# The small expert's up sums: four plain transposes and one VectorE addition in place of products with a constant tile

## The reference

```python
def swiglu(h, w_gate, w_up, w_down):
    a = jnp.einsum('bsd,df->bsf', h, w_gate)
    b = jnp.einsum('bsd,df->bsf', h, w_up)
    return jnp.einsum('bsf,fd->bsd', jax.nn.silu(a) * b, w_down)

def moe_swiglu(h, router, w_gate, w_up, w_down):
    ...
    for e in range(N_EXPERTS):
        y = y + combine[..., e:e + 1].astype(h.dtype) * swiglu(h, w_gate[e], w_up[e], w_down[e])
    return y
```

## Time and profile before

| | |
|---|---|
| median of 3 runs | 1382.0 us (1379.66, 1382.15, 1382.0) |
| the profiled execution | 1379.63 us |
| its span, first to last instruction | 1377.5 us |
| mean granted TensorE clock | 0.998 of full speed |
| moved by DMA | 433.21 MB, 314 GB/s over the span |

### The profile page before, as it was taken

The page is one execution under the profiler, slowest core; times in us unless marked ns, Lnnn a source line. Parts: engine busy times, 40 slices in busy tenths (PEclk is TensorE's granted clock), DMA queues, the critical chain, the costliest instruction groups (busy, mean ns, idle before and its releaser), DMA issues.

```text
span 1377.5 us, 19168 instructions
## 1 busy us (share of the span) xinstructions
PE 1357.2 (99%) x6673; PEld 1095.3 (80%) x6673; DVE 1115.4 (81%) x970; ACT 959.1 (70%) x904; POOL 13.7 (1%) x26
## 2 busy tenths in 40 slices
PE   9999999999999999999999999999999999999997
PEld 7888888888788787877787777787777778787775
DVE  6566544455555789999999999999999999999997
ACT  6554533333454478888887888877888887888886
POOL 1100000000000000000000000000000000000000
PEclk9999999999999999999999999999999999999999
DMA  9813555555351059999999999998999998999993
GB/s 375 319 58 110 212 185 186 194 193 187 131 228 39 17 205 420 422 422 421 422 382 352 421 422 422 422 421 335 399 421 422 422 422 352 379 422 422 422 422 151
DMA packets 61398, 433.21 MB, mean 314 GB/s; under 512 B 7066, under 2 KB 7241, under 8 KB 10032
## 3 DMA queue, kind: packets, MB, share of 16 engines
q1 hardware_dynamic: 59312, 426.80, 76.7%
q0 software_dynamic: 1888, 5.78, 1.2%
q10 hardware_dynamic: 160, 0.14, 0.0%
HBM read 431.60 MB, written 1.09 MB: 314 GB/s over the span
## 4 chain that ended last, share of the span: by engine, by line
PE 95%; DVE 2%; ACT 2%; issue 1%; ACTq 0%; DVEq 0%
PE ps L1453 20%; PE ps L1454 19%; PE ps L1455 19%; PE ps L1851 7%; PE ps L1850 7%; PE ps L1861 4%; PE ps L1862 4%; PE ps L1889 4%; PE ps L1582 1%; PE ps L1786 1%; PE ps L1555 1%; PE ps L1460 1%; PE ps L1853 1%; PE ps L1854 1%; PE ps L1897 1%; PE ps L1823 1%
## 5 line engine op out<-in xcount | busy, mean ns | idle before, releaser
L909 DVE TENSOR_TENSOR wlo<-raw,whi 128x2048 fp32r<-128x2048 f32 (+1 forms) x403 | 905.1, 2283 | 126.1 <-PE ps L1455 90.7
L539 ACT ACTIVATE whi<-raw 128x2048 fp32r<-128x2048 f32 (+1 forms) x403 | 759.0, 1912 | 78.4 <-PE ps L1455 66.3
L1453 PE MATMUL ps<-whi,xhi 128*128 128x512 f32 (+1 forms) x880 | 346.2, 393 | 4.9 <-DVE wlo L909 2.3
L1455 PE MATMUL ps<-whi,xlo 128*128 128x512 f32 (+1 forms) x880 | 342.0, 389 | 0.0
L1454 PE MATMUL ps<-wlo,xhi 128*128 128x512 f32 (+1 forms) x880 | 342.0, 389 | 0.0
L1453 PEld LDWEIGHTS ps<-whi,xhi 128*128 128x128 f32 x880 | 165.2, 188 | 42.1 <-DVE wlo L909 5.2
L1455 PEld LDWEIGHTS ps<-whi,xlo 128*128 128x128 f32 x880 | 165.2, 188 | 34.7
L1454 PEld LDWEIGHTS ps<-wlo,xhi 128*128 128x128 f32 x880 | 165.4, 188 | 32.5
L1851 PE MATMUL ps<-wlo,xhi 128*64 128x512 f32 x392 | 155.2, 396 | 0.0
L1850 PE MATMUL ps<-whi,xhi 128*128 128x512 f32 x392 | 153.4, 391 | 0.0
L1453 PE MATMUL ps<-whi,thi 128*128 128x512 f32 x320 | 125.7, 393 | 0.0
(11 more groups left out here) (248 smaller groups left out, 1102.3 us busy)
## 6 DMA issues: line engine op xcount, KB each, us to landing
raw<-in_moe_up SPq DMA_DIRECT2D x112, 1024.0 KB, 7.4
raw<-in_moe_gate SPq DMA_DIRECT2D x112, 1024.0 KB, 8.0
raw<-in_moe_down SPq DMA_DIRECT2D x112, 1024.0 KB, 7.2
raw<-in_ffn_up SPq DMA_DIRECT2D x14, 1024.0 KB, 4.8
raw<-in_ffn_gate SPq DMA_DIRECT2D x14, 1024.0 KB, 4.8
raw<-in_ffn_down SPq DMA_DIRECT2D x14, 1024.0 KB, 4.8
raw<-in_dil_w_in SPq DMA_DIRECT2D x10, 1024.0 KB, 4.7
raw<-in_swa_w_in SPq DMA_DIRECT2D x4, 1024.0 KB, 19.4
```

The lines of the kernel that those rows point to most:

```text
L539: act.activation(whi[:, c % HIS, 0:span(c)], raw[:, c % RAW, 0:span(c)], ACT.Copy).then_inc(hi_ready, 1)
L909: dve.tensor_tensor(wlo[:, c % LOS, 0:n], raw[:, c % RAW, 0:n], whi[:, c % HIS, 0:n].bitcast(F32), ALU.subtract).then_inc(lo_ready, 1)
L1453: pe.matmul(dst, ahi, bhi, start=start, stop=False)
L1455: return pe.matmul(dst, alo, bhi, start=False, stop=stop)
```

## The change

`fold` no longer multiplies the up sums by the constant tile. It turns them with four plain transposes into bank `B_UB`, which the copies have emptied, and signals `up_turned`. On VectorE a new `small_up` adds the two halves of the turned sums with one reduction: it reads all 512 columns of the bank, in pairs that stand 64 apart, and writes 256 numbers to `small_h` in SBUF. `small_mul` reads them there. The gate sums are folded as before. The transposes wait only for the up sums' copy, the gate products for the gate sums'. TensorE gets two more waits for the addition (`up_added`), because bank `B_UB` is in use until then: ahead of the small up products and in `gather`.

```diff
@@ -285,6 +285,7 @@
         halves_set, sums_out, folded = sem("halves_set"), sem("sums_out"), sem("folded")
+        up_turned, up_added = sem("up_turned"), sem("up_added")
@@ -360,6 +361,14 @@
+        def turned_half(bank, half):
+
+            return ps[:, bank, :].rearrange("p (k t) -> p k t", k=FT)[:, :, half * HALF:(half + 1) * HALF]
+
+        def turned_both(bank):
+
+            return ps[:, bank, :].rearrange("p (k two t) -> p k t two", k=FT, two=2)
@@ -1361,10 +1370,16 @@
+            def small_up(pair, s):
+
+                dve.wait_ge(up_turned, STEPS * pair + s + 1)
+                dve.tensor_reduce(small_act(), turned_both(B_UB), mybir.AxisListType.X, ALU.add).then_inc(up_added, 1)
+
             def small_mul(pair, s):
 
                 dve.wait_ge(silu_b, STEPS * pair + s + 1)
-                dve.tensor_tensor(small_h[:, 1, :], small_folded(0), small_h[:, 0, :], ALU.mult)\
+                dve.wait_ge(up_added, STEPS * pair + s + 1)
+                dve.tensor_tensor(small_h[:, 1, :], small_h[:, 1, :], small_h[:, 0, :], ALU.mult)\
                     .then_inc(act_b, 1)
@@ -1394,8 +1409,9 @@
                     large_tlo(pair, s - 1)
-                    for i in range(1, 3):
-                        cut(c + i, rs)
+                    cut(c + 1, rs)
+                    small_up(pair, s - 1)
+                    cut(c + 2, rs)
                     small_mul(pair, s - 1)
@@ -1409,8 +1425,9 @@
                 large_tlo(pair, STEPS - 1)
-                for i in range(1, 3):
-                    cut(MOE0 + PAIR_UNITS - 4 + i, r)
+                cut(MOE0 + PAIR_UNITS - 3, r)
+                small_up(pair, STEPS - 1)
+                cut(MOE0 + PAIR_UNITS - 2, r)
                 small_mul(pair, STEPS - 1)
@@ -1786,6 +1803,8 @@
+                    if kt == 1 and not first:
+                        pe.wait_ge(up_added, STEPS * pair)
                     if kt == KT - 3 and not first:
                         pe.wait_ge(act_b, STEPS * pair)
@@ -1883,11 +1902,14 @@
             def fold(pair, s):
 
+                pe.wait_ge(sums_out, 2 * (STEPS * pair + s) + 1)
+                for j in range(FT):
+                    last = pe.transpose(ps[:, B_UB, j * P:(j + 1) * P], small_sums(0)[:, j, :], ident)
+                last.then_inc(up_turned, 1)
                 pe.wait_ge(sums_out, 2 * (STEPS * pair + s) + 2)
-                for part in range(2):
-                    for j in range(FT):
-                        last = pe.matmul(small_folded(part)[:, j * HALF:(j + 1) * HALF], small_sums(part)[:, j, :],
-                                         both_halves[:, :], start=True, stop=True)
+                for j in range(FT):
+                    last = pe.matmul(small_folded(1)[:, j * HALF:(j + 1) * HALF], small_sums(1)[:, j, :],
+                                     both_halves[:, :], start=True, stop=True)
                 last.then_inc(folded, 1)
@@ -1926,6 +1948,7 @@
+                    pe.wait_ge(up_added, STEPS * pair + s)
                     for i in range(2):
                         small_in(c + 2 + i, rs, B_UB, i)
```

## The result

| | before | after |
|---|---|---|
| median | 1382.08 us | 1369.34 us |
| runs | 1379.66 to 1383.35 (4) | 1368.19 to 1372.31 (4) |
| profiled execution, its span | 1379.63, 1377.5 us | 1369.4, 1367.6 us |

The ratio is 0.9911, with a 95% interval of 0.9899 to 0.9923: 12.3 us less (10.6 to 14.0). 1369 us had been forecast, in a range of 1366 to 1376.

A forecast was written before the change was run, and what follows sets the result against it. TensorE was taken to bound the kernel, VectorE and transfers within 4%. The fold's 11.8 us, minus 0.4 for new waits, plus 0.6 for the gate sums' wait, minus 0.3 at the end, gave 11.7: forecast 1369 us, range 1366 to 1376.

The forecast's parts named there:

- The bound: Expert steps of 29.72 us: TensorE decides, VectorE and the transfers wait for it, all three within 4%.
- The fold: TensorE, each fold: four transposes replace the up half's products, saving 0.42 us (0.38 to 0.44), 11.8 us over 28 folds.
- New waits: TensorE, ahead of the small up products: waiting for the addition costs its issue alone, 0.4 us in all.
- The gate sums' wait: TensorE at four folds: transposes now stand in front of the 0.8 us wait for gate sums, giving 0.6 us back.
- VectorE's reduction: VectorE, each step: adding the halves takes 0.68 us, 0.60 net; work of 29.09 us fits a 29.30 us step.
- Transfers: Weight transfers don't get faster; in the first pair's last step, transfers and cuts are still in time by 0.3 us.
- The later pairs can't have less: Pairs after the first begin after a pause of the transfers, so their reserve is no smaller than 0.3 us.
- Rival A: Expert steps: the transfers bind, so only 5.9 us are gained, 1373.7 us; chance 0.13.
- The end: Last pair: the last transfer's landing and the cuts behind it hold TensorE's last small products, costing 0.3 us once.
- The sum: Whole kernel: all terms together save 11.7 us, 1367.9 us from the profiled execution; forecast 1369 us, chance 0.70.
- B: Loop steps: VectorE binds from a net reduction of 0.81 us on; 2.4 us gained, 1377.2 us; chance 0.10.
- C: Loop steps: a reduction beyond 1.23 us net, from PSUM pairs 64 apart, makes the kernel slower, 1390 us; chance 0.05.

The follow-up runs named there:

- the first run: VectorE's half of the change on the kernel before: old fold on TensorE, plus the reduction, result unused, and TensorE's waits for it; 1382.19 us, ratio 1.0001.
- half transfers on the kernel before: The kernel before with the weight transfers of the experts' steps at half their bytes, every engine operation kept; 1382.21 us, ratio 1.0003.
- second profile: The unmodified changed kernel profiled again beside the last experiment; 854.77 us from the experts' start to TensorE's last expert product, against 853.86 us in its first profile.

## Why the prediction was right, point by point

**The bound.** "TensorE decides, since the other two wait for it" held, before and after. It is shown by the first run (VectorE's half alone changes nothing) and by half transfers on the kernel before.

**The fold, 0.42 us, mis-sized.** The fold itself gave 0.45 us and the whole step 0.465, both above my upper bound of 0.44. The transposes took 0.43 us as predicted (0.44). The error was in the gate half: I let it give back 0.05 us or nothing, and it fell from 0.87 to 0.82 us. At the first fold of all the halves were 0.87 and 0.87 us, and are 0.43 and 0.81. What a group of transposes takes depends on what comes next. It is 0.43 us ahead of narrow instructions (the gate products, or four more transposes), but 0.36 us for the second four in the run with both kinds of sums transposed, and just as short behind wide products, in `large_t`:

```profile
695.24 0.60 PE L1919 MATMUL ps<-mats,act_h 128*128 128x128 f32 x4
695.59 0.48 PE L1880 MATMUL ps<-wlo,thi 128*64 128x512 f32 x1
```

Both of these stand ahead of a product of 512 columns. Why the gate products cost 0.05 us less behind transposes than behind their like stays open; the whole miss of 0.045 us a step is 1.3 us over 28 folds.

**New waits, -0.4 us.** Nothing: TensorE has no idle time in front of the small up products.

**The gate sums' wait, +0.6 us.** Nothing either. The four folds at the pairs' starts, for which the trace gave 0.8 us of waiting in sum, saved 0.43 to 0.52 us each, the same as all others. So the starts show nothing of the wait that the view listed there, beyond 0.04 us a fold (0.87 us for the up half against 0.83). The view of waits has the 0.8 us at the weight loads (`PEld`) and none at the products.

**VectorE's reduction, 0.68 us and 0.60 net.** It lasts 682 ns, as long as the plain operations on 512 elements, and stands 0.60 us from the next start. The sum 28.49 + 0.60 = 29.09 us a step, which leaves 0.16 us of 29.25, was too high all the same: VectorE pauses twice a step in the kernel before, and each pause leaves the end of an instruction (0.08 us) that otherwise overlaps the next one; the busy time 28.49 holds both. By the distance of starts the work with two reductions is 29.48 us (above), so with one it is 28.88 us, and 0.37 us are left. That it was near the edge is shown by the run with two of them.

**Transfers, in time by 0.3 us in the first pair's last step.** This step of the working failed on a small scale: 0.5 us were lost there. Two things had not been put in. The six folds ahead gained 6 x 0.045 = 0.3 us more, which alone used up the margin. And the transfers did not keep their times: the unit that I had followed landed 183.0 us after the experts' first product, where it was 182.4 us, 0.6 us later. The chain behind the landing was as priced: from 685.18 to the end of the second cut at 692.32 pass 7.1 us, against 7.3. It does not contain the addition, and VectorE stood idle for 0.19 us in it. "The later pairs can't have less" held in one profile and not in the other: the time between the end of a cut and its product, at the same unit of the four pairs, was 0.06, 0.34, 0.52 and 0.68 us, and 0.06, 0.05, 1.13 and 0.40 us in the second profile, where the second pair lost 0.56 us as well. Rival A named the right mechanism, but at 5.8 us, where 0.5 to 1.2 us were lost in the loops.

**The end, 0.3 us.** The weakest term: 1.25 us were lost more than before. I had followed the last transfer alone. What decided came earlier: the unit that landed at 1339.12. From 1341.26 on VectorE worked without a gap, through four cuts and four small operations, until the small part was done at 1352.02:

```profile
1341.26 2.29 DVE L918 TENSOR_TENSOR wlo<-raw,whi 128x2048 fp32r<-128x2048 f32 x1 [0.27 <-ACT whi L548]
1343.47 0.68 DVE L1370 TENSOR_TENSOR tlo<-ps,thi 128x512 fp32r<-128x512 f32 x1
1344.07 2.28 DVE L918 TENSOR_TENSOR wlo<-raw,whi 128x2048 fp32r<-128x2048 f32 x1
1346.27 0.68 DVE L1376 TENSOR_REDUCE small_h<-ps 128x256 f32<-128x512 f32 x1
1346.87 2.28 DVE L918 TENSOR_TENSOR wlo<-raw,whi 128x2048 fp32r<-128x2048 f32 x1
1349.07 0.42 DVE L1382 TENSOR_TENSOR small_h<-small_h 128x256 f32<-128x256 f32 x1
1349.41 2.28 DVE L918 TENSOR_TENSOR wlo<-raw,whi 128x2048 fp32r<-128x2048 f32 x1
1351.61 0.41 DVE L1388 TENSOR_TENSOR thi<-small_h,thi 128x256 fp32r<-128x256 f32 x1
```

The chain had to be summed over everything that VectorE does after a landing, not over the last unit.

**The sum.** 11.7 us had been predicted and 11.2 were found in the trace, by terms that missed in both directions: +1.2 for the fold, +0.4 and -0.6 for the waits, -0.5 and -0.95 for the two places. The mechanism was right, and that the sum came out this close is partly luck. The medians moved by 12.7 us, the ratio says 12.3; the rest lies around the span, as said above, and in the spread of its start. The lower edge of the range had a slip: a saving of 0.44 us and no cost of waits give 1366.7 us, and not 1366.5.

**Rivals.** B (VectorE binds) needed a reduction of over 0.81 us net and C (slower) one of over 1.23; at 0.60 both fall. Made true by hand, with the second reduction, B's mechanism appears, but at half its price. Two reductions are 1.20 us net, by my arithmetic a step of 29.69 us in all loops, 24 x 0.44 = 10.6 us above the changed kernel; 4.7 us were measured. The first pair had mostly 29.43 to 29.52 us, the later ones 29.25 us up to their last steps. The lead at a pair's start and the 0.2 us by which 28.49 was too high were not in it.

## What to carry to other kernels

Where three resources stand within about 4% of each other, a saving on the one that decides pays in full only up to the next one's rate. This change kept 11.2 of its 13.0 us in the traces, and the same edit on the gate sums, with the addition that it needs, made the kernel slower. Price an edit by what it adds to the runner-up as well as by what it takes off the leader, and look at the lead in the last step of a loop, where reserves are gone. At the end of a kernel, add up all the work of the engine behind the last few landings; the last transfer alone says too little. And take a second profile of the same kernel before a microsecond is given to a cause.

## What the runs showed of the hardware

- A reduction on VectorE that reads 512 fp32 elements of PSUM as pairs 64 apart and writes 256 took 682 ns, the time of a plain operation on 512 elements (682 and 683 ns). Neither the stride nor the 256 outputs cost anything that can be seen. The Trainium skill (VectorE: DVE Perf Modes, "Rules for kernel authors") calls this operation the slowest of the engine and says to consider restructuring on a hot path; at this shape no run agrees that it is slower than the others.
- A group of four transposes took 0.43 us ahead of narrow products or other transposes, and 0.35 to 0.36 us ahead of a product of 512 columns, to the start of what came next.
- Transfers of 1 MiB landed every 2.487 us (422 GB/s) inside a pair, before and after, but their time from issue to landing grew (median of the down matrix 7.2 us before, 9.2 after) without one more byte: a transfer issued sooner waited longer behind the others. So a longer time to landing was here no sign of slower transfers.
- The start of the experts' stage, ahead of all code that changed, varied by 3.1 us between profiled executions (500.85 to 503.97). Even from there on two executions of the changed kernel differed by 0.9 us, and the first down unit of a pair's last step was cut 1.13 us ahead of its product in one pair and 0.05 us in another of the same run.
